# A decoder trunk with expert retrieval on one core: the GpSimd queue gathers u of the next group ahead of v of this one

## What is computed

```
ug = u_tab[ids]                                    # 128 rows of u for each token
act = gelu(einsum('td,thkd->thk', xc, ug)) * gate
vg = v_tab[ids]                                    # 128 rows of v for each token
return einsum('thk,thkd->td', act, vg)
```

## Time and profile before

| | |
|---|---|
| device time, three runs | 1835.05, 1836.1 and 1840.62 us, median 1836.1 |
| the profiled execution's own time | 1842.02 us |
| its span in the trace | 1839.1 us |
| mean granted clock of TensorE | 0.905 |
| PE, DVE, ACT, POOL busy | 81%, 63%, 21%, 59% of the span |
| bytes moved by DMA | 649.87 MB, mean 353 GB/s |

### The profile page before, as it was taken

How to read it: one execution, slowest core, us unless ns; L and a number is a source line. 1 busy time by engine, 2 the same in 40 slices (tenths; PEclk the granted TensorE clock), 3 DMA queues, 4 the chain that set the end, 5 groups by cost and what they waited for, 6 DMA issues and landing times.

```text
span 1839.1 us, 15963 instructions
## 1 busy us (share of the span) xinstructions
PE 1493.1 (81%) x4780; PEld 799.9 (43%) x4780; DVE 1157.0 (63%) x2646; ACT 389.9 (21%) x991; POOL 1082.8 (59%) x1028
## 2 busy tenths in 40 slices
PE   6758379889898589889998579879998778777777
PEld 3546235445474234445464234445455433232332
DVE  6644954867469943877468933876648965445453
ACT  2221012233221121233221111233221121111111
POOL 0000345767666655777666655666766667777774
PEclk9768789989998889988999889999998988999889
DMA  7415589989999999999999999999999989999997
GB/s 307 160 35 207 204 359 380 399 297 363 373 401 408 340 418 409 405 369 385 374 401 408 336 415 351 395 340 331 374 376 405 369 301 410 409 409 409 407 388 307
DMA packets 179053, 649.87 MB, mean 353 GB/s; under 512 B 17783, under 2 KB 19319, under 8 KB 174105
## 3 DMA queue, kind: packets, MB, share of 16 engines
q0 software_dynamic: 147456, 536.94, 76.0%
q1 hardware_dynamic: 31512, 111.92, 15.7%
HBM read 644.07 MB, written 4.72 MB: 353 GB/s over the span
## 4 chain that ended last, share of the span: by engine, by line
PE 41%; DVE 32%; DMA 13%; issue 8%; POOL 4%; ACT 2%; DVEq 0%; SPq 0%; POOLq 0%
PE ps L1112 21%; DVE junk L865 12%; DMA ring_u<-table_u,ids 11%; PE ps L934 8%; PE ps L1069 3%; POOL ring_v L1143 2%; PE ps L1082 2%; DMA ring_v<-table_v,ids 1%; PE ps L999 1%; POOL ring_u L1138 1%; DVE W L690 1%; DVE W L842 1%; DVE W L844 1%; DVE W L845 1%; PE ps L1009 1%
## 5 line engine op out<-in xcount | busy, mean ns | idle before, releaser
L1112 PE MATMUL ps<-ring_v,diag 128*128 128x512 f32 x2048 | 982.4, 636 | 229.2 <-ACT diag L480 227.6
L865 DVE CUSTOM_DVE_ANT_0 junk<-ring_u,h 128x1024 bf16<-128x1024 f32 x512 | 627.4, 1225 | 268.1 <-DMA ring_u<-table_u,ids 212.5
L1138 POOL DMA_INDIRECT ring_u<-table_u,ids x512 | 536.1, 1047 | 387.7 <-DVE ids L849 204.9
L1143 POOL DMA_INDIRECT ring_v<-table_v,ids x512 | 546.5, 1067 | 352.2 <-PE ps L1112 269.9
L1112 PEld LDWEIGHTS ps<-ring_v,diag 128*128 128x128 f32 x2048 | 412.0, 205 | 761.4 <-issue 751.6
L471 ACT ACTIVATE acts<-dots 128x4 f32<-128x4 f32 x128 | 26.3, 205 | 998.6 <-DVE dots L865 998.6
L480 ACT ACTIVATE diag<-cst,weights 128x128 f32<-128x128 f32 x512 | 163.5, 390 | 39.2 <-DVE weights L874 39.0
L934 PE MATMUL ps<-W,hT 128*128 128x384 f32 (+2 forms) x384 | 142.9, 531 | 4.0 <-DVE hT L576 2.6
L1082 PE MATMUL ps<-hT,W 128*128 128x128 f32 x1024 | 117.7, 276 | 2.7 <-DVE hT L576 2.6
L1082 PEld LDWEIGHTS ps<-hT,W 128*128 128x128 f32 x1024 | 116.0, 192 | 3.8 <-DVE hT L576 3.8
L934 PEld LDWEIGHTS ps<-W,hT 128*128 128x128 f32 x384 | 73.7, 193 | 72.3 <-issue 36.9
(11 more groups left out here) (247 smaller groups left out, 1050.4 us busy)
## 6 DMA issues: line engine op xcount, KB each, us to landing
W<-w_in SPq DMA_DIRECT2D x32, 1282.0 KB, 15.2
W<-peer_wq SPq DMA_DIRECT2D x16, 2048.0 KB, 21.0
W<-w_out SPq DMA_DIRECT2D x4, 4096.0 KB, 19.5
ring_u<-table_u,ids POOLq DMA_INDIRECT x512, 7.8
ring_v<-table_v,ids POOLq DMA_INDIRECT x512, 7.7
W<-keys_t SPq DMA_DIRECT2D x4, 1024.0 KB, 8.3
zkv<-gain_mix SPq DMA_DIRECT2D x4, 512.0 KB, 16.0
toep<-ring_u SPq DMA_DIRECT2D x1, 2048.0 KB, 7.4
```

Of the source, the lines that this page charges most:

```text
L865: v.tensor_tensor_reduce(junk[:, :], ring_u[:, s, :], h[:, b, :], 1.0, 0.0, ALU.mult, ALU.add, dots[:, s:s + 1]).then_inc(dots_done, 1)
L1112: mm = pe.matmul(ps[:, c, :], diag[:, s, :], ring_v[:, s, c * 512:(c + 1) * 512], start=False, stop=False, skip_group_check=True)
L1138: gp.indirect_dma_start(ring_u[:, k % RING, :], None, table_u, bass.IndirectOffsetOnAxis(ap=ids[:, b, k:k + 1], axis=0)).then_inc(u_in[k % ...
L1143: gp.indirect_dma_start(ring_v[:, k % RING, :], None, table_v, bass.IndirectOffsetOnAxis(ap=ids[:, b, k:k + 1], axis=0)).then_inc(v_in[k % ...
```

## The change

GpSimd's list of gathers is put in another order. Before, it was four of u and four of v of group 0, then four of u and four of v of group 1, and so on. Now it is four of u of group 0, four of u of group 1, four of v of group 0, four of u of group 2, four of v of group 1, and so on to the end, where the last two groups of v follow each other. Each gather keeps its own waits, its slot and its semaphore; the number of gathers, the rings and all other engines' programs stay.

```
-            for n in range(PASSES):
-                b = n % NB
-                for i in range(HALVES):
...
-                    for k in range(RING_G * i, RING_G * (i + 1)):
-                        if m >= 2:
-                            gp.wait_ge(dots_done, SLOTS * n + k - RING + 1)
-                        gp.indirect_dma_start(ring_u[:, k % RING, :], None, table_u,
...
-                    for k in range(RING_G * i, RING_G * (i + 1)):
-                        if m >= 2:
-                            gp.wait_ge(v_used, SLOTS * n + k - RING + 1)
-                        gp.indirect_dma_start(ring_v[:, k % RING, :], None, table_v,
...
+            def rows_of_u(t):
+                n, i = t // HALVES, t % HALVES
+                if i % (HALVES // 2) == 0:
+                    gp.wait_ge(ids_ready, 2 * n + i // (HALVES // 2) + 1)
+                for k in range(RING_G * i, RING_G * (i + 1)):
+                    if t >= 2:
+                        gp.wait_ge(dots_done, SLOTS * n + k - RING + 1)
+                    gp.indirect_dma_start(ring_u[:, k % RING, :], None, table_u,
...
+            def rows_of_v(t):
...
+                    if t >= 2:
+                        gp.wait_ge(v_used, SLOTS * n + k - RING + 1)
+                    gp.indirect_dma_start(ring_v[:, k % RING, :], None, table_v,
...
+            rows_of_u(0)
+            for t in range(PASSES * HALVES):
+                if t + 1 < PASSES * HALVES:
+                    rows_of_u(t + 1)
+                rows_of_v(t)
```

More of the change, by code:

```diff
@@ L1128, in _ @@
             gp.wait_ge(s5_out, 16 * (DEPTH - 1))
-            for n in range(PASSES):
-                b = n % NB
-                for i in range(HALVES):
-                    if i % (HALVES // 2) == 0:
-                        gp.wait_ge(ids_ready, 2 * n + i // (HALVES // 2) + 1)
-                    m = HALVES * n + i
-                    for k in range(RING_G * i, RING_G * (i + 1)):
-                        if m >= 2:
-                            gp.wait_ge(dots_done, SLOTS * n + k - RING + 1)
-                        gp.indirect_dma_start(ring_u[:, k % RING, :], None, table_u,
-                                              bass.IndirectOffsetOnAxis(ap=ids[:, b, k:k + 1], axis=0)).then_inc(u_in[k % RING], 16)
-                    for k in range(RING_G * i, RING_G * (i + 1)):
-                        if m >= 2:
-                            gp.wait_ge(v_used, SLOTS * n + k - RING + 1)
-                        gp.indirect_dma_start(ring_v[:, k % RING, :], None, table_v,
-                                              bass.IndirectOffsetOnAxis(ap=ids[:, b, k:k + 1], axis=0)).then_inc(v_in[k % RING], 16)
+            def rows_of_u(t):
[6 more added lines that the diff above has]
+                    gp.indirect_dma_start(ring_u[:, k % RING, :], None, table_u,
+                                          bass.IndirectOffsetOnAxis(ap=ids[:, n % NB, k:k + 1], axis=0)).then_inc(u_in[k % RING], 16)
+            def rows_of_v(t):
+                n, i = t // HALVES, t % HALVES
+                for k in range(RING_G * i, RING_G * (i + 1)):
+                    if t >= 2:
+                        gp.wait_ge(v_used, SLOTS * n + k - RING + 1)
+                    gp.indirect_dma_start(ring_v[:, k % RING, :], None, table_v,
+                                          bass.IndirectOffsetOnAxis(ap=ids[:, n % NB, k:k + 1], axis=0)).then_inc(v_in[k % RING], 16)
+            rows_of_u(0)
[3 more added lines that the diff above has]
+                rows_of_v(t)
 def shape_constants():
```

## The result

The changed kernel took 1865.24 us (median of 4 runs, 1861.85 to 1870.94) beside 1835.57 us for the kernel before (4 runs): a ratio of 1.0166, 95% interval 1.0123 to 1.0209. Run again later it took 1863.84 us (6 runs) beside 1841.56 (23 runs): 1.0122, 1.0099 to 1.0145. So it is slower, by 22 to 30 us. I had forecast 1851.6 us, 15.5 more than before, with a range up to 1864.

What follows compares the result with a forecast made beforehand. GpSimd and DMA set the pace in pass 3; in passes 0 to 2 PE and DVE take turns. 5 + 12 + 4 - 5 - 0.5 = 15.5 us on 1836.1 gave 1851.6 us, range 1834 to 1864.

Steps and rivals of the forecast that it cites:

- the three places: Groups 1, 31 and 63, where v was to land late in a w_in load: losses of 5, 12 and 4 us.
- The start, +5: Group 1: its v, now behind the first u of group 2, falls into the w_in load; loss 5 us.
- Pass 0 into 1, +12: Groups 31 and 32: v of 31 lands in the w_in load behind u of 32; loss 12 us.
- Pass 1 into 2, +4: Groups 63 and 64: v of 63 lands late in a smaller w_in load; loss 4 us.
- Gains, -5: Group 24 of three passes: DVE's waits for u under the peer_wq loads go, together -5 us.
- Query steps, 0: Passes 0 to 2 outside the w_in loads: v is just on time behind u; cost taken as 0.
- slower by more: Rival, chance 0.14: v also late in the query steps, 5 us in each of three passes; 30 us slower, 1867.
- Pass 2 into 3 has no load ... I take -0.5 us for it and the whole of pass 3: Crossing into pass 3 and all of it: GpSimd's waits shrink a little, pace stays 10.3 us a group; -0.5 us.
- There u is late in two kinds of places only: Passes 0 to 2: u late only at group 24 of a pass and the first group of passes 1 and 2.
- a sign of being wrong: Group 31: v landing less than 25 us after its issue would show the forecast wrong.
- No change: Rival, chance 0.17: gathers get half of DMA beside a load, 2.5 us each; -0.5 us, 1836.
- faster: Rival, chance 0.11: u's lead outweighs v's, if a gather in the load takes under 2.3 us; -14 us, 1822.

Runs made afterwards that it cites:

- after_late_load: Changed kernel, but SP starts the w_in loads for passes 2 and 3 only after the running pass's dots: 1875.35 us, 1.0205 of the kernel before.
- all_but_three: Kernel before with the new order everywhere except at groups 1, 31 and 63, which keep the old one: 1851.89 us, ratio 1.0082.
- after_again: The changed kernel itself run again, with more runs of the kernel before beside it: 1863.84 us, ratio 1.0122.
- passes012: Kernel before with the new order in passes 0 to 2 and the old one from group 96 on: 1861.34 us, ratio 1.0118.
- quiet_groups: Kernel before with the new order in passes 0 to 2 except groups 0, 1, 31, 32, 63 and 64: 1844.13 us, ratio 1.0010.
- query_only: Kernel before with the new order only at groups 22, 23, 54, 55, 86 and 87: 1836.97 us, ratio 1.0002.
- pass3_only: Kernel before with the new order from group 96 on, the old one in passes 0 to 2: 1841.67 us, ratio 1.0011.
- short_dots_old: Kernel before, old order, with DVE's dots in pass 3 reading only the first 64 of 1024 columns: 1835.73 us, ratio 0.9975.
- three_places: Kernel before with the new order at groups 1, 31 and 63 alone: 1863.67 us, ratio 1.0131.
- both kernels with short dots: Kernel before with pass 3 dots of 64 columns, in the old order (1835.73 us) and with the new order from group 96 on (1830.82 us).

## Why the prediction came out too low

The direction, the three places and their cause were right; 1865.24 us lies 13.6 above the forecast and 1.2 above the range. The step that failed is the one on pass 3, and a term for TensorE's clock was missing. Step by step:

- **The start, +5:** measured +5.8, +5.8, +6.2, +6.0 and (after_late_load) +7.5 in the five traces that have it, and 0.0 in all_but_three. Right.
- **Pass 0 into 1, +12:** 10.1 and 9.3. The mechanism was right. PE ended group 32's matmuls at 691.7, against 690.8 in the forecast. One detail was off: DVE's dots were to end near 660 and ended at 665.5, since the first u of 32 landed at 651.2 and not at 645.8. It left 3 us later than I had it (641.18), behind a start that was already 2.8 us late. Nor did the sum see that v of 32 behind u of 33 would cost as much without v of 31; both overlap, so by luck the total hardly suffered. The landings of v of 31 took 21.4 to 26.5 us; I had named less than 25 as a sign of being wrong, a mark that my own places (from 643 to 663.2, 20 us) didn't keep.
- **Pass 1 into 2, +4:** 5.4 and 5.2. Right.
- **Gains, -5:** -4.2 in after, after_again, passes012 and quiet_groups, and alone in query_only. Right, a little less than the waits that went (5.4).
- **Query steps, 0:** PE waited 3.61 and 1.41 us for v there (from 566 us on), but it didn't reach DVE. The rival "slower by more" named 1867 us, near the result, but its mechanism didn't occur.
- **"Pass 2 into 3 has no load ... I take -0.5 us for it and the whole of pass 3":** this step failed. It rests on a pace of 10.3 us that I read from two issues of one execution and took for fixed. In the profiled execution of after this part cost 12.6 us and in after_again 2.1. The runs show that 10.3 us is the least that DMA allows, and that above it the pace depends on how many issues are stretched beside DVE's dots; the order's own share is 2 to 3 us by the means and not told from zero.
- **"There u is late in two kinds of places only":** misread, though no term of the sum hangs on it. In passes 0 to 2 DVE waited 74.5 us for u, and the two kinds make 33 of them; the rest stands at groups 3 and 4 (14.3), 34 to 36 (15.8) and 67 and 68 (10.7).
- **A missing term of 3 to 5 us:** groups 14 to 23 took 2.9 us longer in four of the five traces with the late start, and 1.7 in the fifth (after_late_load). It comes up where TensorE comes out of a pause of 3.9 us, ahead of group 14's matmuls with v. PE in before, and then in after:

```profile
430.06 0.65 PE L1023 MATMUL ps<-cst,W 128*128 128x128 f32 x4 [3.87 <-DVE W L731]
...
434.01 7.03 PE L1112 MATMUL ps<-ring_v,diag 128*128 128x512 f32 x16
```

```profile
431.62 1.11 PE L1023 MATMUL ps<-cst,W 128*128 128x128 f32 x4 [3.86 <-DVE W L731]
...
438.36 7.03 PE L1112 MATMUL ps<-ring_v,diag 128*128 128x512 f32 x16
```

After the same pause, the same twenty matmuls of the mixing step take 6.74 us instead of 3.95 until L1112 can start: TensorE is for a while at the lower of its two levels (mean granted clock from 432 to 440 us 0.67 instead of 1.00). The work is the same and only its time has shifted. Where the start isn't late this stretch costs 0 to 0.2 us in six traces and 1.8 in two (pass3_only, short_dots_old; in pass3_only the same twenty matmuls take 5.64 us). So a late start is not the only thing that does it, and that a late start must do it was not shown. The +1.7 to +2.0 of groups 69 to 80 are of the same size in kernels that don't have the change (-2.4 to +2.9) and I don't assign them.

Together: 5.8 + 10 + 5.3 - 4.2 are 17 us for what I had put at 16; the clock adds 3, groups 69 to 80 perhaps 2, and pass 3 adds 2 to 3 as a rule and 13 in the execution that I have the trace of. That makes 22 to 25 us, which is what the 23 runs of before give (22.3) and three_places too (24.5), though that has neither the gains nor the new order in pass 3. That the four-run comparison gave 29.7 lies mostly in the kernel before: the medians of after differ by 1.4 us (1865.24 and 1863.84), those of before by 6.0 (1835.57 from 4 runs, 1841.56 from 23). Why pass 3 was so long in the profiled execution of after stays open.

The other rivals. "No change" wanted half of DMA for the gathers, and "faster" less than 2.3 us a gather: both fell with the 4.37 us between dots in after, unchanged although fewer gathers were queued. The page of the Trainium skill that I had set against the row ("DMA: Bandwidth & Descriptors", section on queues, rings and completion order: the queues are served in turn, packet by packet) thus doesn't give the share here by itself; 120 of 421 GB/s stayed 29%. I had read it as an even share, which needs even packets, and the packets were not compared.

## What to carry to other kernels

When one queue issues for two consumers, each wait for the one holds the other's transfers back: ask not which consumer waits longer in total, but what lies ready in each ring at the moment a bulk load begins, since a gather costs 4.4 us in it and 1.3 outside. Read a total such as DVE's 212.5 us by place before acting on it; here 137.9 of them stood in pass 3, where DMA and GpSimd set the pace, and the order won back only 14. And take a pace from several executions before writing "unchanged" beside a quarter of the program.

## What the runs showed of the hardware

- An indirect gather takes GpSimd 0.94 us to issue while DVE does no full dot (0.95 at most in groups 98 to 127 of every trace), and 1.01 to 1.11 us on average, 1.99 at most, beside the dots with two inputs of 1024 columns. With 64 columns it stays 0.94 (0.99 at most). The Trainium skill ("SBUF — State Buffer", section "Who interferes with whom") says that a DVE instruction with two SBUF inputs contends with a GpSimd instruction that reads SBUF; the summary of rules on the same page says that the second to issue is blocked until the first is done. The traces agree that they contend; of being blocked for a whole dot of 1.23 us they show little, as most stretched issues are 0.13 us longer, and only 3 to 19 of 232 exceed 1.2 us.
- DMA moved 409 GB/s in pass 3, at a share of 1.03, in before and in both kernels with short dots. Issuing a group in 10.0 instead of 10.4 us brought the data no sooner (10.35 us a group); it raised the time from issue to landing from 7.8 to 13.7 us.
- A load that SP starts 12 to 15 us later costs the old order nothing (1.0000) and makes the new one 7 to 14 us slower, though both move the same bytes.
- TensorE's clock can cost 2.8 us in one place in a kernel that does the same work after the same pause (3.95 or 6.74 us for twenty matmuls after 3.9 us of idling). It did so in four of the five traces in which that stretch came later, for 1.7 us in the fifth, and for 1.8 in two in which it came no later.
